# A two-layer decoder trunk on one Trainium2 core: three moves in the hand-written order of its first pass

## The reference, cut to what matters

```python
h = rms_norm(x, norm_mix[layer])
z = h @ w_in[layer]                      # 1024 x 2564: q, k, v of three attentions, f, s5 input
...                                      # fox_o, dil_o, diff_o, s5_o from z
x = x + concat([fox_o, dil_o, diff_o, s5_o]) @ w_out[layer]
# peer, in chunks of 128 tokens
q = (xc @ wq).reshape(c, 8, 2, 128)
sc = einsum('thpd,hpkd->thpk', q, keys)  # top 16 of each half, then of their 256 sums
ug = u_tab[ids]; act = gelu(einsum('td,thkd->thk', xc, ug)) * gate
x = x + einsum('thk,thkd->td', act, v_tab[ids])
```

## Time and profile before

| | |
|---|---|
| median of 3 runs | 1621.42 us (1619.0 to 1621.73) |
| the profiled execution's own time | 1621.11 us |
| its span, first to last instruction | 1619.3 us |
| around the span | 1.8 us |
| PE busy | 1425.6 us (88%) |
| DVE busy | 1130.5 us (70%) |
| ACT busy | 465.7 us (29%) |
| moved by DMA | 632.09 MB, 390 GB/s over the span |

### The profile page before, as it was taken

How to read it: one execution, slowest core, us unless ns; L and a number is a source line. 1 busy time by engine, 2 the same in 40 slices (tenths; PEclk the granted TensorE clock), 3 DMA queues, 4 the chain that set the end, 5 groups by cost and what they waited for, 6 DMA issues and landing times.

```text
span 1619.3 us, 15416 instructions
## 1 busy us (share of the span) xinstructions
PE 1425.6 (88%) x4754; PEld 771.8 (48%) x4754; DVE 1130.5 (70%) x2797; ACT 465.7 (29%) x1127; POOL 591.1 (37%) x525
## 2 busy tenths in 40 slices
PE   7898788999999799788998799899898988777778
PEld 4667344554475344344465444455456533333333
DVE  5825998876657798784557888787456796765554
ACT  3522224352322224342221232444212222221112
POOL 1002333554323234354442333455452433333332
PEclk9989898999999899999999999999999989989999
DMA  9357898999999999999999999999999999999997
GB/s 364 147 194 310 346 410 324 419 381 420 418 412 418 420 409 373 417 421 419 421 415 395 423 421 421 421 405 390 420 418 411 374 397 422 421 420 422 421 421 330
DMA packets 103134, 632.09 MB, mean 390 GB/s; under 512 B 9697, under 2 KB 10977, under 8 KB 35214
## 3 DMA queue, kind: packets, MB, share of 16 engines
q0 software_dynamic: 74144, 537.97, 80.9%
q1 hardware_dynamic: 28910, 93.14, 14.8%
HBM read 630.01 MB, written 1.06 MB: 390 GB/s over the span
## 4 chain that ended last, share of the span: by engine, by line
PE 50%; DMA 22%; DVE 17%; issue 6%; ACT 3%; another core or an unknown queue 1%; SPq 0%; POOL 0%; POOLq 0%; DVEq 0%; ACTq 0%
PE ps L1577 30%; DMA ring<-table_uv,ids 20%; PE ps L1544 7%; DVE ring L1217 6%; PE ps L1357 3%; PE ps L1522 3%; DMA W<-peer_wq 2%; ACT acts L729 1%; ACT diag L752 1%; PE ps L1471 1%; PE ps L1424 1%; DVE W L995 1%; DVE W L1192 1%; DVE W L1190 1%
## 5 line engine op out<-in xcount | busy, mean ns | idle before, releaser
L1577 PE MATMUL ps<-ring,diag 128*128 128x512 f32 x2016 | 937.3, 620 | 143.0 <-ACT diag L752 135.4
L1629 POOL DMA_INDIRECT ring<-table_uv,ids x512 | 585.4, 1143 | 990.7 <-PE ps L1577 851.2
L1577 PEld LDWEIGHTS ps<-ring,diag 128*128 128x128 f32 x2016 | 392.6, 199 | 637.1 <-issue 626.2
L1217 DVE CUSTOM_DVE_ANT_0 ring<-ring,h 128x1024 f32<-128x1024 f32 x384 | 456.6, 1223 | 165.7 <-DMA ring<-table_uv,ids 163.4
L729 ACT ACTIVATE acts<-dots,small 128x4 f32<-128x4 f32 x126 | 37.6, 298 | 851.9 <-DVE dots L1217 824.1
L1217 DVE CUSTOM_DVE_ANT_0 ring<-ring,ps 128x1024 f32<-128x1024 f32 x120 | 144.7, 1220 | 95.3 <-DMA ring<-table_uv,ids 94.8
L752 ACT ACTIVATE diag<-cst,weights 128x128 f32<-128x128 f32 x504 | 161.6, 392 | 29.2 <-DVE weights L1226 29.0
L1544 PE MATMUL ps<-hT,W 128*128 128x128 f32 x960 | 114.6, 282 | 13.8 <-DMA W<-peer_wq 13.7
L1544 PEld LDWEIGHTS ps<-hT,W 128*128 128x128 f32 x960 | 113.4, 198 | 17.9 <-issue 17.8
L1357 PE MATMUL ps<-W,hT 128*128 128x512 f32 (+2 forms) x256 | 95.2, 527 | 2.7 <-DVE hT L869 2.7
L1357 PEld LDWEIGHTS ps<-W,hT 128*128 128x128 f32 x256 | 48.5, 190 | 52.0 <-issue 47.4
(11 more groups left out here) (291 smaller groups left out, 1162.1 us busy)
## 6 DMA issues: line engine op xcount, KB each, us to landing
W<-peer_wq SPq DMA_DIRECT2D x13, 2048.0 KB, 32.0
W<-w_in SPq DMA_DIRECT2D x16, 1282.0 KB, 14.6
W<-w_out SPq DMA_DIRECT2D x8, 2048.0 KB, 18.5
ring<-table_uv,ids POOLq DMA_INDIRECT x512
W<-w_in SPq DMA_DIRECT2D x8, 898.0 KB, 8.4
W<-w_in SPq DMA_DIRECT2D x4, 1024.0 KB, 11.6
ring<-w_in SPq DMA_DIRECT2D x2, 1544.0 KB, 19.1
ring<-w_in SPq DMA_DIRECT2D x2, 1536.0 KB, 21.1
```

The source lines that it names most:

```text
L1217: v.tensor_tensor_reduce(ring_u[:, r, :], ring_u[:, r, :], tokens, 1.0, 0.0, ALU.mult, ALU.add, dots[:, s:s + 1]).then_inc(dots_done, 1)
L1577: mm = pe.matmul(ps[:, c, :], diag[:, s, :], ring_v[:, r, c * 512:(c + 1) * 512], start=(k == 0), stop=(k == SLOTS - 1), skip_group_check= ...
L1629: gp.indirect_dma_start(ring[:, t % RING, :], None, table_uv, bass.IndirectOffsetOnAxis(ap=ids[:, b, k:k + 1], axis=0)).then_inc(pair_in[t ...
```

## The change

Three moves in the lists of `plan_steps`; no instruction's operands change, and none is added or removed.
1. "tables 0" goes from the end of the first list to the end of the second, behind "z 0". On DVE the 27 instructions thus follow the eviction of bank 0.
2. "next columns 3", "4" and "5" go into the attention: behind "heads 1", "y 0" and "y 1". Columns 6 and 7 take the places of 3 and 4 around "rows 1", and "next z" follows them, ahead of "square 1". The place between "quick 0" and "query 5" is then empty.
3. "query 3" and "score 3" go behind "dots 0 0" and "weigh 0 0". PE has no part in those two, so its order stays; on ACT the copy of query 3 now follows the first gelu and its four diagonals.

```diff
-    first = [["rows 0", "steps 0", "lines", "square 0", "phases 0", "sines 0", "mean 0", "tables 0"],
-             ["columns 0", "columns 1", "columns 2", "columns 3", "z 0"],
+    first = [["rows 0", "steps 0", "lines", "square 0", "phases 0", "sines 0", "mean 0"],
+             ["columns 0", "columns 1", "columns 2", "columns 3", "z 0", "tables 0"],
...
-             ["keys 2", "next columns 2", "weights 2", "heads 1", "inverse 2"],
+             ["keys 2", "next columns 2", "weights 2", "heads 1", "next columns 3", "inverse 2"],
              ["heads 2", "logits 6", "co sums"],
-             ["logits 7", "y 0", "softmax 3", "co scale"],
-             ["weights 3", "y 1", "s5 out", "inverse 3"],
+             ["logits 7", "y 0", "next columns 4", "softmax 3", "co scale"],
+             ["weights 3", "y 1", "next columns 5", "s5 out", "inverse 3"],
              ["heads 3", "gate rows"],
              ["glu", "mixed rows 0"],
              ["out 0", "gated", "mixed rows 1", "out 1", "out 2", "out 3"],
-             ["next columns 3", "rows 1", "next columns 4", "square 1", "gain", "query 4", "mean 1", "score 4"],
-             ["quick 0", "best 4", "pairs 4", "next columns 5", "next columns 6", "next columns 7", "next z", "query 5", "score 5", "query 1", "score 1", "ids 4", "query 2", "score 2", "best 5", "pairs 5",
-              "query 3", "score 3"]]
+             ["next columns 6", "rows 1", "next columns 7", "next z", "square 1", "gain", "query 4", "mean 1", "score 4"],
+             ["quick 0", "best 4", "pairs 4", "query 5", "score 5", "query 1", "score 1", "ids 4", "query 2", "score 2", "best 5", "pairs 5",]]
...
             if i == 0 and n:
                 plan.append(("gathered", n - 1, 0))
+            if n == 0 and i == 0:
+                do(["query 3", "score 3"], n)
             if i == 0:
                 plan.append(("rows of v", n, i))
```

## The result

| us | before | after |
|---|---|---|
| median of the first five runs of each | 1619.0 us (1613.49 to 1621.73) | 1608.69 us (1605.63 to 1613.38) |
| profiled execution, its span | 1621.11, 1619.3 us | 1609.26, 1607.4 us |
| start of "bu" of pass 0 | 37.41 | 41.83 |
| start of "bu" of pass 1 | 257.96 | 246.63 |
| from there to the end of the span | 1361.3 | 1360.8 |

The ratio is 0.9939, 95% interval 0.9919 to 0.9959: faster by 0.6%, some 10 us. Two later measurements of the same kernel gave 0.9952 (0.9933 to 0.9970) and 0.9943 (0.9928 to 0.9957).

What follows compares the result with a forecast made beforehand. Engines were taken to bound the early kernel, transfers the part from 400. Terms 2.8 + 0.56 + 0 + 1.29 - 3.87 - 4.6 - 4.4 = -8.2 took 1621.1 to 1612.9 us; range 1610 to 1619.5.

Steps and rivals of the forecast that it cites:

- The bound: Whole kernel: engines bound the early part, transfers the part from 400; every microsecond won ahead of 160 reaches the end.
- The rival that the transfers absorb it: From 400 on: transfers set the end, a better head only lengthens gather waits; no change, 1621.1 us, chance 0.09.
- Part 1, +2.8: Kernel head: tables behind bank 0's eviction delay "turned 0" by 2.2 us, plus 0.6 at half clock; ends +2.2 and +4.2.
- -3.87: Before query 5: the three column steps that stood there leave the chain, saving 3.87 us.
- Columns 3 and 4, +0.56: Attention: column 3 behind "heads 1" delays "heads 2" by 0.56 us; column 4 fits PE's idle 1.30 us, costing 0.
- Column 5 and the clock, 1.29 - 4.6 = -3.3: Attention's end, 83.2 to 93.4: column 5 costs 1.29 us; PE keeping full clock saves 4.6, ends -4.8 and 0.
- Part 3, -4.4: First dots: gelu ahead of query 3's copy lets "ids 5" go on at 157.85 instead of 162.25, saving 4.4 us.
- the rule on table changes: Table load before "ids 5": the skill page adds a drain of about 1380 ns, making the -4.4 term -3.0.
- The clock as before: Rival, at 83: PE's clock still falls, column 5 costs 2.58 and the -4.6 is gone; -2.3, 1618.8 us, chance 0.18.
- binding gathers: Rival, first pass: dots come 4.4 us sooner, their gathers only 1.1; total -4.9, 1616.2 us, chance 0.12.
- a clock already down at "heads 2": Rival, 77 to 93: PE enters "heads 2" at half clock, "weights 3" 7.5 later; +4.6 in all, 1625.7 us, chance 0.06.
- neither moved nor priced: Query 1, around 131 to 134: PE stops 2.4 us with nothing to wait for; taken as 0, ends -2.4 and +2.4.

## Why the prediction was right and where it was wrong

- *The bound.* Right: what is won ahead of 160 reaches the end. The rival that the transfers absorb it is refuted by the table above: heads up to 19 us apart (257.96 and 239.24), the same rest.
- *Part 1, +2.8.* Right: "bu" starts 2.85 later on the mean of three traces each. In the first trace it was 4.4, 1.2 of it because bank 0 was done only at 27.0 (25.2 and 25.4 in the two others, 25.8 computed).
- *Part 2.* -3.87: the distance from the projection to the copy of query 5 fell from 30.51 to 26.63, -3.88. Columns 3 and 4, +0.56: "bu" to "weights 3" grew from 45.96 to 46.36, +0.4. Column 5 and the clock, 1.29 - 4.6 = -3.3: 11.07 to 7.77 us, -3.3. That column 4 alone can hold the clock (one trace) I hadn't seen; I named both. The forecast had one length for the clock's fall; in two of four traces of the old order it was 13.6 us and not 10.2, which cost 1.3 more.
- *Part 3, -4.4.* Right: 6.69 to 2.25 us, -4.44. One detail was off: the table load of the gelu waited for the dots, so that DVE waited 1.70 us before the first weights and 0.44 before the second part of "ids 5" (forecast: 1.7 in the second place). So too the diagonals end 1 us later behind the dots than I said, and the margin ahead of query 3's end was 1.2 us instead of 2.2. It cost nothing. Of the rule on table changes (the Trainium skill, ScalarE: Activation LUTs, "What ACT_TABLE_LOAD costs") the trace again bears out the 1.28 us of the load and not the drain: 0.02 us between load and exponential, and the term came out as the rows had it.
- *The rivals.* The clock as before, binding gathers, transfers, a clock already down at "heads 2": none occurred.
- *The step that failed* is the one under "neither moved nor priced": PE's stop in query 1, "I take 0, with ends of -2.4 and +2.4". Two errors are in it. I took a stop that waits for nothing as a property of the kernel, while it belonged to that execution. And I sized it by its idle time of 2.4 us, whereas it took 4.2: the clock fell behind it, and 3.4 us of query 1 ran at 0.50 (134.4 to 137.8). The range's lower end, 1610.0, held only 2.4 for this. With the stop gone and at its real size, 1621.1 - 8.2 - 4.2 = 1608.7, the measured median.
- *What of that is luck.* That it comes out to 0.1 us. The second execution of the kernel before had no stop and still took 1620.29, since the rest took 1364.5 in it; a sum made on that one would still have been 3.4 too high. The difference stands on more: the heads of the three traces of the kernel before, less the 4.2 of the stop in the first, end at 253.4 on average, those of the changed kernel at 244.9, 8.5 apart for the 8.2 of the sum, and the rest averages 1361.2 in both. By the three ratios the gain is 9.9, 7.8 and 9.2 us. Against 1617.32, the median of 28 runs of the kernel before that were made beside the first experiments, the same -8.2 gives 1609.1. So the forecast difference was right, and the time from which it was subtracted was one high execution.

## What to carry to other kernels

Before a sum is made on one profiled execution, look for pauses on the critical engine that wait for nothing, and price them at the distance between the steps around them, half clock included, not at the idle time. Better still, trace the kernel two or three times: the forecast of a difference is safer than that of a time. Work of the matrix engine that is free to move was worth most here in a gap next to thin work, where the clock stayed up with it. A part of a change that only moves a stall ahead of its own consumer (the tables) should be tried alone, since here it took back 3 of some 12 us.

## What the runs showed of the hardware that I had not expected

- The pause in query 1: up to 1.83 us between two weight loads (1.13 between two products) in a stream of 64 products without waits, then half clock, 4.2 us in all, in one of thirteen traces.
- The spread of the same kernel from run to run, 1609.3 to 1625.0 us in 28 runs, is larger than the whole change; in three traces of the kernel before, 5.7 us of it stood ahead of 258 (252.29 to 257.96) and 6.7 behind (1357.8 to 1364.5).
- PE lost its clock without standing idle for long: from 79.7 to 83.2 it was busy for 2.2 to 2.7 of 3.5 us, mostly with products of 32 columns and with no gap over 1.3 us, and the clock fell at 83.1 to 84.7 in each of the four traces of that order. That it is the width of the products, and not their number or the gap, was not tried by itself.
